# Smaller first transfers and a row read from PSUM: both ends of a two-block decoder kernel

## The chip, the cores and the metric

One core of a Trainium2 chip. The metric is the device time in microseconds (us) of one execution. The engines are TensorE (PE; its weight loads are shown apart as PEld), VectorE (DVE), ScalarE (ACT), GpSimd (POOL) and the sequencer that issues most DMAs (SyncE, SP).

## The reference

Two small language-model blocks, one after the other, on one sequence of 256 tokens with 1024 channels, all in float32. The first block puts 16 meta tokens in front (272 tokens) and has two layers: latent attention (8 heads) and a gated linear recurrence. The second has two layers of attention (differential, then ordinary causal) with a memory attention, and an MLP with a squared relu:

```
h = concatenate([meta, x]);  h = h + mla_mixer(rmsnorm(h, g) @ w_in ...)    # first block
...
u = relu(h @ w_up);  h = h + (u * u) @ w_down                               # end of the last layer
out = rmsnorm(h, final_norm_2) = h * rsqrt(mean(h * h) + 1e-6) * final_norm_2
```

## The kernel before, in words

The residual stream lies in SBUF with channels on partitions: 8 tiles of 128 channels by 272 (later 256) tokens. The weights come from DRAM as 252 units, 512 KB each but for a few, in the order of their use. A weight W is split into a rounded part `weights_hi` (ACT, L1016) and the rest `weights_lo` (DVE, L1449); the input is split likewise (`operand_hi`, `operand_lo`). A product is three matmuls (L666 hi*hi, L667 hi*lo, L668 lo*hi), so a unit of 8 tiles costs TensorE 24 matmuls of 272 or 256 columns. There are 5 buffers for raw units and 6 for split ones; ACT waits before it splits unit v until unit v-6 has been multiplied.

Every engine runs a fixed list of steps. `timetable()` (L240) makes the lists for ACT and DVE by sorting steps by the numbers of the table `TIMES` (L157): a step with the number 8.5 stands between the split of unit 8 and that of unit 9. TensorE's list follows the units, with the statistics and attention steps at fixed places between them. An engine works through its list strictly in order, so a step whose input is late holds all that stand behind it.

Start. SP issues the gains (`vec`), then in turn two input tiles (272 KB) and half a unit (256 KB), four times, then units 2 to 4 and the constants (L2014 to L2023). ACT and DVE split input tiles and weight halves in that order (`input_a`, `split_weights(piece=i)`, L1419 to L1423, L1949 to L1954); then ACT squares the tiles and splits units 2, 3 and 4 in between, while DVE adds the squares up. TensorE multiplies units 0 and 1 (`tile_by_inputs`, L697): for each of two output tiles, over four input tiles. The first norm ("a"): `mean` (L852) on TensorE behind unit 3, `root` (L1048) on ACT, `rstd` on DVE, `spread` (L867) on TensorE behind unit 4, `row` (L1042) on ACT. `row` copies a row of per-token factors from a PSUM bank into SBUF.

End. The last eight units are the `down` projection (L779): output tiles 2j and 2j+1 share a PSUM bank. After each pair DVE adds it to the residual (`residual_pair`), ACT squares it, DVE adds the squares. After the last unit: the same for tiles 6 and 7, `total`, `mean`, `root`, `rstd`, `spread`; ACT multiplies all eight tiles by the gain (L1436 to L1440), copies the row, DVE multiplies three pairs by it, POOL the tiles 6 and 7 one by one, and SP writes five pieces.

## Time and profile before

| | |
|---|---|
| median of 3 runs | 844.8 us (844.73 to 845.4) |
| the profiled execution | 846.0 us, span of its instructions 844.2 us |
| TensorE busy | 818.6 us, 97% of the span, 6612 matmuls |
| DVE / ACT busy | 560.8 us / 532.3 us |
| DMA | 137.39 MB, 163 GB/s over the span |
| first matmul / last residual add | 7.83 us / 832.12 us from the span's start |

Times in the profile count from the span's start. A busy TensorE says only that a matmul was in its pipeline; the pace is the distance between two starts. Idle time of an engine is listed with what ended it.

### The profile page before, as it was taken

The numbers are of one execution on the slowest core, as the hardware profiler recorded it, in microseconds if no ns is written. First come the engines' busy times: TensorE is split into PE (matmuls) and PEld (weight loads), VectorE is DVE, ScalarE is ACT, GpSimd is POOL, SyncE is SP. The second block draws the span as 40 slices with busy tenths as digits, with TensorE's granted clock in tenths as the row PEclk, the third lists the DMA queues.
The fourth block names the chain that finished last, engine by engine and source line by source line (L and its number), as shares of the span: only waits on it lengthen the run. The fifth ranks groups of instructions, "written<-read, shape, count | busy, mean of one in ns | idle before, by whom it ended". The sixth has DMA issues, their size and how long they took to land.

```text
span 844.2 us, 16068 instructions
## 1 busy us (share of the span) xinstructions
PE 818.6 (97%) x6612; PEld 786.2 (93%) x6612; DVE 560.8 (66%) x1004; ACT 532.3 (63%) x962; POOL 2.6 (0%) x6
## 2 busy tenths in 40 slices
PE   6999999999999998899999999999999999999994
PEld 6997769999999898899999999999899999999994
DVE  6685658889988976567536553876758656465353
ACT  6478766589977868763544545668867546444442
POOL 0000000000000000000000000000000000000001
PEclk9999999999999999999999999999999999999998
DMA  8453215555745432445645764444336737374431
GB/s 313 150 188 113 63 51 172 191 162 210 231 170 170 124 124 98 155 171 166 221 163 181 250 193 150 150 151 144 107 108 217 242 119 253 113 258 167 148 101 50
DMA packets 41448, 137.39 MB, mean 163 GB/s; under 512 B 4384, under 2 KB 8736, under 8 KB 41376
## 3 DMA queue, kind: packets, MB, share of 16 engines
q1 hardware_dynamic: 41376, 136.37, 49.0%
q8 instruction: 52, 0.85, 0.4%
q14 instruction: 20, 0.16, 0.1%
HBM read 135.31 MB, written 1.05 MB: 162 GB/s over the span
## 4 chain that ended last, share of the span: by engine, by line
PE 94%; DVE 3%; ACT 1%; DMA 1%; issue 0%; DVEq 0%; ACTq 0%; SPq 0%
PE bank L666 26%; PE bank L668 26%; PE bank L667 25%; PE bank L671 2%; PE bank L939 2%; PE bank L672 2%; PE bank L673 2%; PE bank L891 1%; PE bank L892 1%; DVE temp L1449 1%; PE bank L860 1%; DVE residual L1449 1%; PE bank L919 1%; DMA weights_raw<-stream_dram 1%; PE bank L920 1%; DVE weights_lo L1449 1%
## 5 line engine op out<-in xcount | busy, mean ns | idle before, releaser
L666 PE MATMUL bank<-operand_hi,weights_hi 128*128 128x256 f32 (+1 forms) x1860 | 529.5, 285 | 10.9 <-DVE weights_lo L1449 7.8
L668 PE MATMUL bank<-operand_hi,weights_lo 128*128 128x256 f32 (+1 forms) x1860 | 526.7, 283 | 0.0
L667 PE MATMUL bank<-operand_lo,weights_hi 128*128 128x256 f32 (+1 forms) x1860 | 526.6, 283 | 0.0
L666 PEld LDWEIGHTS bank<-operand_hi,weights_hi 128*128 128x128 f32 x1860 | 352.4, 189 | 16.3 <-DVE weights_lo L1449 8.7
L668 PEld LDWEIGHTS bank<-operand_hi,weights_lo 128*128 128x128 f32 x1860 | 352.8, 190 | 0.0
L667 PEld LDWEIGHTS bank<-operand_lo,weights_hi 128*128 128x128 f32 x1860 | 350.8, 189 | 0.0
L1016 ACT ACTIVATE weights_hi<-weights_raw 128x1024 fp32r<-128x1024 f32 (+2 forms) x254 | 258.3, 1041 | 130.1 <-PE bank L668 92.5
L1449 DVE TENSOR_TENSOR weights_lo<-weights_raw,weights_hi 128x1024 fp32r<-128x1024 f32 (+2 forms) x254 | 298.5, 1205 | 52.5 <-ACT weights_hi L1016 52.4
L1449 DVE TENSOR_TENSOR operand_lo<-temp,operand_hi 128x512 fp32r<-128x512 f32 (+2 forms) x48 | 28.4, 601 | 55.0 <-ACT operand_hi L1016 55.0
L1455 DVE SCALAR_TENSOR_TENSOR temp<-bank,rows 128x512 f32<-128x512 f32 x32 | 21.9, 688 | 40.6 <-PE bank L668 39.7
L671 PE MATMUL bank<-weights_hi,operand_hi 128*128 128x256 f32 (+1 forms) x140 | 41.6, 297 | 0.0
L1028 ACT ACTIVATE temp<-temp 128x512 f32<-128x512 f32 x32 | 19.9, 621 | 33.8 <-DVE temp L1455 33.8
L673 PE MATMUL bank<-weights_hi,operand_lo 128*128 128x256 f32 (+1 forms) x140 | 40.7, 291 | 0.0
L672 PE MATMUL bank<-weights_lo,operand_hi 128*128 128x256 f32 (+1 forms) x140 | 40.6, 290 | 0.0
L1016 ACT ACTIVATE operand_hi<-residual,vectors 128x256 fp32r<-128x256 f32 (+1 forms) x48 | 22.4, 505 | 21.2 <-DVE residual L1449 21.1
L1016 ACT ACTIVATE arena<-bank 128x512 f32<-128x512 f32 (+3 forms) x46 | 22.4, 500 | 19.0 <-PE bank L668 14.1
L1449 DVE TENSOR_TENSOR residual<-residual,bank 128x512 f32<-128x512 f32 (+1 forms) x28 | 17.1, 614 | 25.9 <-PE bank L668 25.6
L1016 ACT ACTIVATE operand_hi<-temp 128x512 fp32r<-128x512 f32 (+2 forms) x48 | 26.7, 560 | 6.2 <-DVE temp L1449 5.1
L1028 ACT ACTIVATE temp<-residual 128x512 f32<-128x512 f32 (+1 forms) x36 | 18.7, 530 | 17.1 <-DVE residual L1449 14.9
L1455 DVE SCALAR_TENSOR_TENSOR operand_lo<-residual,vectors,operand_hi 128x256 fp32r<-128x256 f32 (+1 forms) x48 | 21.5, 486 | 10.8 <-ACT operand_hi L1016 10.7
L1282 ACT ACTIVATE temp<-temp,softmax_stats 128x128 f32<-128x128 f32 (+1 forms) x48 | 21.4, 450 | 11.3 <-DVE softmax_stats L1814 11.3
L671 PEld LDWEIGHTS bank<-weights_hi,operand_hi 128*128 128x128 f32 x140 | 26.4, 188 | 1.5 <-issue 1.0
(177 smaller groups left out, 645.3 us busy)
## 6 DMA issues: line engine op xcount, KB each, us to landing
weights_raw<-stream_dram SPq DMA_DIRECT2D x244, 512.0 KB, 4.4
weights_raw<-stream_dram SPq DMA_DIRECT2D x6, 384.0 KB, 3.5
temp<-memT_dram SPq DMA_DIRECT2D x8, 256.0 KB, 3.4
residual<-xT_dram SPq DMA_DIRECT2D x4, 272.0 KB, 4.9
weights_raw<-stream_dram SPq DMA_DIRECT2D x4, 256.0 KB, 5.1
out_dram<-residual SPq DMA_DIRECT2D x3, 256.0 KB, 2.2
constants<-consts_dram SPq DMA_DIRECT2D x1, 536.0 KB, 7.8
out_dram<-residual SPq DMA_DIRECT2D x2, 128.0 KB, 2.1
```

Source lines behind the costliest of these rows:

```text
L666: e.matmul(to, w_h, x_h, start=start, stop=False, skip_group_check=True)
L667: e.matmul(to, w_h, x_l, start=False, stop=False, skip_group_check=True)
L668: return e.matmul(to, w_l, x_h, start=False, stop=stop, skip_group_check=True)
L671: e.matmul(to, x_h, w_h, start=start, stop=False, skip_group_check=True)
L672: e.matmul(to, x_h, w_l, start=False, stop=False, skip_group_check=True)
L673: return e.matmul(to, x_l, w_h, start=False, stop=stop, skip_group_check=True)
L939: mm = e.matmul(bank[b][:, at:at + nk], qt[p0:p0 + DH, q0:q0 + nq], kt[p0:p0 + DH, 0:nk], start=True, stop=True, skip_group_check=True)
L1016: return e.activation(to, of, ACT.Copy, bias=0.0, **scale)
L1028: return e.activation(to, of, ACT.Square, bias=0.0, scale=scale)
L1282: e.activation(prob[:, at:at + nk], src, ACT.Exp, bias=st[:, 4 * j:4 * j + 1], scale=-1.0, accum_out=st[:, 4 * j + 1:4 * j + 2]).then_inc( ...
L1449: return e.tensor_tensor(to, a, b, op)
L1455: return e.scalar_tensor_tensor(to, a, s, b, op0, op1)
```

## The change

Start: the first input tiles and the first half unit are transferred one by one; the gains and the input tiles 2, 3 and 6, 7 are issued from ACT's own queue, the rest from SP's. A copy of one column on ACT, which needs no input from DRAM, stands ahead of the first input split. TensorE begins with five matmuls of zeros, and in units 0 and 1 the loop over inputs is outside that over the two output tiles. End: tiles 6 and 7 are added and squared one by one (tile 7 in a bank of its own); ACT multiplies by the gain in its list, ahead of and between the last steps; the mean is summed from two parts in PSUM; there is no `row` copy, DVE reads the row from PSUM for four pairs; POOL does nothing; each tile is written on its own, from SP and ACT in turn. Beside that, every number of `TIMES` is new: most steps of ACT and DVE between the splits stand at another place. TensorE's list is the same.

```diff
+WARM = 5
+FIRST_WEIGHTS = [(0, 0, 256), (0, 256, 256), (0, 512, 512), (1, 0, 512), (1, 512, 512)]
+FIRST_TILES = [(0, 1), (1, 1), (2, 2), (4, 2), (6, 2)]
...
+def at_last(w):
+
+    return w.kind == "down" and w.layer == 1 and w.k0 == 24 and w.m0 > 5
...
 TIMES = {
-    ("scalar", "root"): (7.67, 12.29, 12.14, 32.6, 34.67, 74.33, 101.5, 163.67, 194.25),
+    ("scalar", "root"): (8.25, 11.4, 11.8, 33.25, 35.67, 75.33, 99.75, 163.67, 194.33),
...
-    ("vector", "sub_mean"): (87.25, 91.33),
+    ("vector", "sub_mean"): (87.12, 92.25),
...
+    ("scalar", "gained"): (251.23, 251.54, 251.62, 251.46, 251.69, 251.31, 251.77, 251.92),
...
# tile_by_inputs
+                for k in range(4):
+                    pe.wait_ge("weights_piece", first_weights_of(v, k))
+                    wait_input(v, w.k0 + k)
+                    for j, b in enumerate(bank_of(v)):
                         w_h, w_l = weights(v, k, j)
...
+            def mean_out():
+
+                take(6)
+                for k, part in enumerate((temp[0][:, 0:SEQ], temp[2][:, SEQ:512])):
+                    pe.wait_ge(*(("square", "d1", 7) if k else ("total", "out")))
+                    for i in range(2):
+                        mm = e.matmul(bank[6][:, i:i + 1], part[:, i * P:(i + 1) * P], ones[:, 0:1],
+                                      start=k == 0 and i == 0, stop=k == 1, skip_group_check=True)
...
+            pe.wait_ge("zeros")
+            for _ in range(WARM):
+                e.matmul(bank[7][:, 0:SEQ], temp[6][:, 0:P], temp[6][:, P:P + SEQ], start=True, stop=True)
...
# scalar
+            e.dma_start(vec[:], vecs).then_inc(*done("vectors_landed", ("vectors",), by=16))
+            load_tiles(2)
+            act.wait_ge("eps")
+            copy(cols[:, 21:22], EPS_COL, scale=1.0)
+            load_tiles(4)
...
-            for k in range(DT):
-                act.wait_ge("x_added", "d1", k - k % 2)
-                copy(xs[:, k, :], xs[:, k, :], scale=vcol("final_norm_2", k)).then_inc(*done("x_gained", ("x_gained", k)))
-                if k == 1:
-                    root("out")
-            row("out")
+            root("out")
+            for k in range(1, DT, 2):
+                act.wait_ge("out", k - 1)
+                e.dma_start(out[k * P:(k + 1) * P, :], xs[:, k, :]).then_inc(*done("output_written_act", ("written", k), by=16))
...
# vector
+            def residual_last(k):
+                dve.wait_ge("sum", "down", 1, k, 24)
+                tt(xs[:, k, :], xs[:, k, :], bank[3 if k == 6 else 7][:, 0:SEQ], ALU.add).then_inc(
...
-            dve.wait_ge("row", "out")
-            row = RC.unsqueeze(1).to_broadcast([P, 2, SEQ])
-            for k in (0, 2, 4):
-                dve.wait_ge("x_gained", k + 1)
+            dve.wait_ge("spread", "out")
+            row = bank[6][:, P:P + SEQ].unsqueeze(1).to_broadcast([P, 2, SEQ])
+            for k in range(0, DT, 2):
+                for kk in (k, k + 1):
+                    dve.wait_ge("x_gained", kk)
                 tt(xs[:, k:k + 2, :], xs[:, k:k + 2, :], row, ALU.mult).then_inc(*done("outputs", ("out", k)))
```

## Rows read from the trace of the kernel before

**Rows 1.** The page, part 1: engine, busy us, share, instructions.

```profile
PE 818.6 (97%) x6612; PEld 786.2 (93%) x6612; DVE 560.8 (66%) x1004; ACT 532.3 (63%) x962; POOL 2.6 (0%) x6
```

**Rows 2.** The page, part 4: shares of the chain that ended last, by engine.

```profile
PE 94%; DVE 3%; ACT 1%; DMA 1%; issue 0%; DVEq 0%; ACTq 0%; SPq 0%
```

**Rows 3.** Waits of TensorE, 60 to 832 us, first and last of six: total us, times, longest.

```profile
PE bank L666 <- DVE operand_lo L1455: 3.1, 3, 1.7
...
PE bank L891 <- ACT arena L1016: 0.5, 1, 0.5
```

**Rows 4.** Timeline of the start: start us, duration, engine, line, what [idle before].

```profile
4.30 1.28 ACT L1016 ACT_TABLE_LOAD   x1 [4.30 <-DMA residual<-xT_dram]
5.18 0.67 SPq L1994 DMA_DIRECT2D weights_raw<-stream_dram  x1
7.83 0.59 PE L666 MATMUL bank<-operand_hi,weights_hi 128*128 128x272 f32 x1 [7.83 <-DVE weights_lo L1449]
```

**Rows 5.** DMA issued at 5.18 us (unit 2): KB, us to landing.

```profile
weights_raw<-stream_dram SPq DMA_DIRECT2D x1, 512.0 KB, 6.4
```

**Rows 6.** Chain of waits, start of the kernel: start us, us, what.

```profile
8.42 0.23 PE bank L667
13.83 0.13 PE bank L667
```

**Rows 7.** Timeline of ACT and DVE, 11 to 26 us.

```profile
11.69 1.04 ACT L1016 ACTIVATE weights_hi<-weights_raw 128x1024 fp32r<-128x1024 f32 x1
17.55 0.43 ACT L1028 ACTIVATE temp<-residual 128x272 f32<-128x272 f32 x1 [1.07 <-DVE temp L1449]
17.89 3.89 ACT L1016 ACTIVATE weights_hi<-weights_raw 128x1024 fp32r<-128x1024 f32 x4
...
11.37 0.68 DVE L1449 TENSOR_TENSOR weights_lo<-weights_raw,weights_hi 128x512 fp32r<-128x512 f32 x1
12.84 1.23 DVE L1449 TENSOR_TENSOR weights_lo<-weights_raw,weights_hi 128x1024 fp32r<-128x1024 f32 x1 [0.43 <-ACT weights_hi L1016]
15.94 1.23 DVE L1449 TENSOR_TENSOR weights_lo<-weights_raw,weights_hi 128x1024 fp32r<-128x1024 f32 x1 [0.51 <-ACT weights_hi L1016]
```

**Rows 8.** Timeline of TensorE: start of unit 2, mean and spread of norm "a".

```profile
16.57 0.29 PE L666 MATMUL bank<-operand_hi,weights_hi 128*128 128x272 f32 x1
...
22.62 0.72 PE L860 MATMUL bank<-constants,temp 128*128 128x1 f32 x6
23.20 0.37 PE L666 MATMUL bank<-operand_hi,weights_hi 128*128 128x272 f32 x1
...
26.41 0.59 PE L876 MATMUL bank<-constants,cols 16*128 16x16 f32 x3
```

**Rows 9.** Chain of waits: a float32 matmul of 272 columns, two instructions.

```profile
69.50 0.65 PE bank L892 x2
```

**Rows 10.** Groups of DVE, 0 to 832 us: busy us, mean ns of one | idle.

```profile
L1449 DVE TENSOR_TENSOR residual<-residual,bank 128x272 f32<-128x272 f32 x8 | 3.5, 435 | 2.1 <-PE bank L668 2.0
```

**Rows 11.** Timeline of the end, all engines.

```profile
832.12 0.69 DVE L1449 TENSOR_TENSOR residual<-residual,bank 128x512 f32<-128x512 f32 x1 [3.60 <-PE bank L668]
834.71 0.61 PE L860 MATMUL bank<-constants,temp 128*128 128x1 f32 x4 [2.70 <-DVE temp L1449]
835.36 0.26 ACT L1059 ACTIVATE cols<-bank,cols 128x2 f32<-128x2 f32 x1 [1.08 <-PE bank L860]
835.96 0.44 PE L876 MATMUL bank<-constants,cols 128*128 128x128 f32 x2 [0.64 <-DVE cols L1513]
838.30 0.69 DVE L1449 TENSOR_TENSOR residual<-residual,rows 128x512 f32<-128x512 f32 x1 [2.49 <-ACT rows L1016]
838.35 1.23 POOL L1986 TENSOR_TENSOR residual<-residual,rows 128x256 f32<-128x256 f32 x1 [837.91 <-ACTq L472]
838.91 1.21 DVE L1449 TENSOR_TENSOR residual<-residual,rows 128x512 f32<-128x512 f32 x1
```

**Rows 12.** Page, part 6: output DMAs, KB each, us to landing.

```profile
out_dram<-residual SPq DMA_DIRECT2D x2, 128.0 KB, 2.1
```

More of the change, by code:

```diff
@@ L403, in timetable @@
             vector("finish", v)
+    end = AT["down", 1, 24, 0]
+    for m in range(8):
+        scalar("gained", m)
+    vector("total_out")
     return {engine: [step for _, _, step in sorted(rows)] for engine, rows in table.items()}
@@ L593, in bank_of @@
             if w.kind == "down":
-                return [w.m0 // 2]
+                return [7 if w.layer == 1 and w.m0 == 7 else w.m0 // 2]
             if w.kind == "up":
@@ L709, in tile_by_inputs @@
                                   w.k0 + k == 0, w.k0 + k == 7)
-                    i.then_inc(*done("sums", ("sum", w.kind, w.layer, j), ("unit", v)))
-                    held_by[b] = [("evacuated", w.kind, w.layer, j)]
+                        if k == 3:
+                            i.then_inc(*done("sums", ("sum", w.kind, w.layer, j), ("unit", v)))
+                            held_by[b] = [("evacuated", w.kind, w.layer, j)]
             def tiles(v, T, t0=0, base=0):
@@ L782, in down @@
                 pe.wait_ge("weights_lo", v)
-                (b,), j = bank_of(v), w.m0 % 2
+                (b,), j = bank_of(v), 0 if w.layer == 1 and w.m0 == 7 else w.m0 % 2
                 if w.k0 == 0 and j == 0:
@@ L865, in mean @@
                     mean("in2_0g")
+            def mean_out():
[5 more added lines that the diff above has]
+                                      start=k == 0 and i == 0, stop=k == 1, skip_group_check=True)
+                mm.then_inc(*done("statistics_sums", ("mean", "out")))
+                held_by[6] = [("mean_read", "out")]
             def spread(name):
@@ L1239, in squares_pair, with d1_squares, last_squares, gained @@
                 square(pair(to), xs[:, m:m + 2, :]).then_inc(*done("squares", ("square", name, m)))
+            def d1_squares(m):
+                act.wait_ge("x_added", "d1", m)
+                squares_pair("d1", m)
+            def last_squares(k):
+                act.wait_ge("x_added", "d1", k)
+                act.wait_ge("square_read", "d1", 4)
+                square(temp[2][:, (k - 6) * SEQ:(k - 5) * SEQ], xs[:, k, :]).then_inc(
+                    *done("squares", ("square", "d1", k)))
+            def gained(k):
+                act.wait_ge("square", "d1", k if k > 5 else k - k % 2)
+                copy(xs[:, k, :], xs[:, k, :], scale=vcol("final_norm_2", k)).then_inc(*done("x_gained", ("x_gained", k)))
             def squares_gained(m):
@@ L1757, in residual_pair, with total_out @@
                     *done("residual", ("x_added", name, m), ("evacuated", step[0], step[1], m + 1)))
+            def residual_last(k):
+                dve.wait_ge("sum", "down", 1, k, 24)
+                tt(xs[:, k, :], xs[:, k, :], bank[3 if k == 6 else 7][:, 0:SEQ], ALU.add).then_inc(
+                    *done("residual", ("x_added", "d1", k), ("evacuated", "down", 1, k)))
+            def total_out():
+                dve.wait_ge("square_read", "d1", 4)
+                linked(tt(temp[0][:, 0:SEQ], temp[0][:, 0:SEQ], temp[0][:, SEQ:512], ALU.add))
+                dve.wait_ge("square", "d1", 6)
+                tt(temp[0][:, 0:SEQ], temp[0][:, 0:SEQ], temp[2][:, 0:SEQ], ALU.add).then_inc(
+                    *done("square_sums", ("total", "out")))
             def residual_pair_rest(name, m, o, gain, *ready):
@@ L1946, in bank_of_tile @@
                 return m if m < 2 else bank_of(AT["a_in", 0, 0, m])[0]
+            e.memset(temp[6][:, 0:P + SEQ], 0.0).then_inc(*done("statistics", ("zeros",)))
             e.memset(EPS_COL, EPS).then_inc(*done("statistics", ("eps",)))
@@ L2029, in sync @@
                 load_weights(v)
[L2030 to L2031 removed]
+            for k in range(0, DT, 2):
                 sp.wait_ge("out", k)
[L2033 removed]
+                load(out[k * P:(k + 1) * P, :], xs[:, k, :], "output_written",
                      "written", k)
[L2035 removed]
+            sp.wait_ge("written", 6)
         tally.begin(known=False)
[L2039 removed]
+        for body in (sync, scalar, vector, tensor):
             body(Rehearsal())
```

200 lines of the change are left out of this document (103 added, 97 removed), and 36 rows, old and new, of the table TIMES.

## The prediction

> **What bounds the kernel now.** I read the page first. TensorE is busy 97% of the span [rows 1] and makes up 94% of the chain that ended last [rows 2], so between the ends time is the pace of its matmuls, which the change leaves alone. The waits of TensorE come next: between 60 and 832 us there are eight, in six rows of which the first and the last stand in [rows 3]; with 0.8, 0.8, 0.7 and 0.5 us of the four between they come to 6.4 us, the longest 1.7. That is all that a new order of ACT's and DVE's steps could win back there. Then the two ends. At the start TensorE stands still for 7.83 us; ACT waits until 4.30 us for the first input tiles and only then loads its function table, 1.28 us [rows 4]. After the start the pace is 0.23 us a matmul, later 0.13 us [rows 6]: 272 columns in 0.227 us are 1.2 GHz, in 0.125 us nearly 2.4 GHz; it changes near 13.5 us, 5.7 us after the first matmul. At the end, 12.1 us of the span (844.2 - 832.12) lie behind the last residual add [rows 11].
>
> **The start, until unit 2.** The first input tile is now 136 KB at the head of its queue, and the table load lies beside its transfer, so ACT can begin near 3.5 us instead of 5.60. The table load (1.28 us) and most of a us of landing go. But TensorE has to be followed to where it next runs without waiting. Unit 2 is issued at 5.18 us and lands 6.4 us later, at 11.6 [rows 4, 5]; ACT splits it at 11.69, 1.04 us, DVE from 12.84 to 14.07 [rows 7]. Nothing of the bytes ahead of it has changed (gains, eight tiles, units 0 and 1 come to 2.2 MB either way), so I leave 14.07 as it is. TensorE began unit 2 at 16.57 [rows 8]. It can now begin at 14.1, if units 0 and 1 are through: 2.5 us gained, no more.
>
> Are they through? Their last piece was split by 12.05 (11.37 + 0.68) [rows 7]; with ACT's earlier start I take 11.6. It feeds 12 matmuls, 1.5 us at 0.125: done at 13.1. That needs the fast pace. The five matmuls of zeros start near 1.1 us. A float32 matmul of 272 columns took 0.65 us at the fast pace [rows 9], so one of 256 takes 0.61, and up to 1.22 at the slow one: together 3.1 to 6.1 us. The trace shows none at the slow pace; the ordinary matmul grew 1.8 times, which gives 5.5 us, until 6.6. If the clock rises again 5.7 us after the first activity, it does so near 6.9 and nothing of units 0 and 1 is late. If the zeros do not count, real matmuls start at 6.6, 31 of the 48 run at 0.227 until 13.6, the other 17 end at 15.7: 0.9 us gained. The loop turned round costs nothing by itself (same 48 matmuls) and lets TensorE use a piece as it comes.
>
> The Trainium skill, "DMA: Bandwidth & Descriptors", section "Issuing engines are not separate DMA queues", says that DMAs of several issuers interleave on the same 16 engines, and that a second issuer saves only issue time. It speaks against a gain from the second queue; since the sum above takes none for unit 2, it is the same by that rule. The section "Bandwidth" adds that small transfers move fewer bytes a second; no row here compares 136 with 272 KB. If it cost unit 2's landing half a us, the start would win that much less.
>
> **The start, after unit 2.** Unit 3 is ready at 17.17 (15.94 + 1.23) [rows 7]; TensorE wants it at 14.07 + 3.02 = 17.09: 0.1 us lost. It ends at 20.2, `mean` takes 0.58 (22.62 to 23.20), unit 4 takes 3.21 (23.20 to 26.41) [rows 8]: TensorE wants `spread` at 24.0. Here the new list bites. `root` of norm "a" stood ahead of the split of unit 8 (7.67), now behind it (8.25). ACT splits units 4 to 7 from 17.89 to 21.78 without a pause [rows 7]; unit 8 at that rate (0.95 each) ends at 22.7. Table load 1.28 [rows 4], root 0.26 and 0.34 from its end to the start of the spread, as at the end of the kernel (835.62 to 835.96) [rows 11]: `spread` at 24.6 against 26.41, a gain of 1.8 us. DVE's split of unit 7 waits behind `rstd`, but is wanted only at 31. ACT's copy of the row follows at once, so the banks of units 0 and 1 are free before unit 6 wants one. Behind that everything is relative to TensorE. **Start: 1.8 us**; bounds 0.9 - 0.6 = 0.3 (clock low and ACT late) and 2.9 (unit 2 lands 0.4 earlier, root in time).
>
> **The middle.** Nothing is added for TensorE. A step of ACT or DVE moved by one split comes about 1.0 us (ACT) or 1.2 us (DVE) earlier or later [rows 7]. The lists move both ways: `sub_mean` of the second group from 91.33 to 92.25, behind unit 92's split; `root` of norm "in2_0" from 74.33 to 75.33; but the first memory softmax on DVE from 74.67 to 73.5. TensorE waits only where a chain is short of time, and the eight waits follow directly on work that TensorE itself had just finished, so much of each is plain latency that no order removes. I take zero; bounds: half of the waits gone (-3.2), three more splits in front of a wait (+3.2).
>
> **The end.** From 832.12, in the new order: add of one tile 0.44 [rows 10]; square of one tile on ACT 0.43, as at 17.55 [rows 7]; two matmuls of the mean 0.61, the first part having been summed under the last unit's wake; root 0.26; 0.34 to the spread, 0.44 for it [rows 11]. With five handovers of 0.03 that is 834.8, against 838.30 for DVE's first product before. What goes: half an add, half a square, the two sums of squares (833.5 to 834.7) and, the largest, the wait for ACT's six gain copies and the row copy: the spread was there at 836.4, DVE began at 838.30. These copies now lie under the last unit: five of them 2.1 us between unit 250's square and the end, the eighth behind the last square and beside the mean, so `root` is not held. Then four products instead of three with two on POOL. DVE's product took 0.69 alone and 1.21 beside POOL's [rows 11]; one that reads PSUM took 0.69 too (the add at 832.12), so four take 2.5 us at a pitch of 0.60 (838.30 to 838.91): 837.3. The last two tiles go out on two queues, landing 2.1 us after the issue [rows 12], 839.4; the span ended 0.4 us behind the last landing: 839.8 against 844.2. **End: 4.4 us.** Bounds: 3.4 (an ACT-issued write lands half a us later and the tiny matmuls run at the low clock, as they did when the row shows 0.44 at 835.96) and 4.9 (smaller pieces land sooner).
>
> **Sum.** 1.8 + 0 + 4.4 = 6.2 us. The profiled execution took 846.0 us, span 844.2; the same 6.2 off the median of the runs, 844.8, gives 838.6.
>
> **Rivals.**
> 1. *The new lists also shorten TensorE's waits.* For: 6.4 us are there [rows 3], and steps such as the first softmax stand earlier. Against: each wait follows a handover chain of its own. Half of them: 838.6 - 3.2 = 835.4.
> 2. *The start gives nearly nothing*: clock low through units 0 and 1, as computed 0.9 instead of 2.5 us, and ACT late for `root`: 844.8 - 4.4 - 0.3 = 840.1. The Trainium skill, "TensorE: Matmul & The Clock Gate", section "The HAM clock gate", says that activity releases the throttle; by that rule the zeros count and this rival falls; the rows show only a rise 5.7 us behind the first matmul.
> 3. *The lists cost a part of the gain*, one to four splits in front of waiting steps (1 to 5 us): about 841.6.
> 4. *Slower.* One split more in front of the step that TensorE waits for, at each of the eight places of rows 3 (units 18 to 97, the attention of the layers): 8 x 1.05 = 8.4 us against 6.2, 847.0. It decides from six places on. For: `sub_mean` 91.33 to 92.25 and `root` 74.33 to 75.33 are such moves. Against: others go the other way.
> 5. *The smaller first transfers do not land sooner*: ACT then starts at 4.3, and unit 2 still sets the pace; the time stays within 0.3 us of the forecast, so it has no case of its own.
>
> **How the numbers follow.** Forecast 0.52, rival 1 0.18, rival 2 0.12, rival 3 0.12, rival 4 0.06. The forecast alone would lie in 837.3 to 839.9. The range reaches to rival 1 and rival 3: 835.0 to 841.8. About 0.2% (1.7 us) can be told from no change. Faster needs more than 1.7 of 6.2 us to stay: all cases but rival 4 and the worst of rival 3. Faster 0.92, same 0.03, slower 0.05.
>
> **What would show it.** Unit 2 begins near 14.1 us and `spread` of norm "a" near 24.6; the pace at the first real matmul 0.125 us (else rival 2). Between unit 5 and the last, the same distance as before, with eight waits of about 6 us. From the last add to the end 7.7 us, DVE's first product 2.6 us behind the add and no product above 0.7 us. I am wrong if the waits of TensorE in the middle differ from 6.4 us by more than 1, or if unit 2 lands well ahead of 11.6.

## The result and the profile after

| | before | after |
|---|---|---|
| median of the runs | 845.3 us (6 runs, 844.73 to 845.76) | 840.2 us (6 runs, 838.93 to 841.47) |
| profiled execution, its span | 846.0, 844.2 us | 838.93, 837.1 us |
| mean granted clock of the span | .995 | .997 |
| TensorE waits between unit 5 and the last | 6.4 us, eight | 6.0 us, nine |
| last residual add to the span's end | 12.1 us | 8.1 us |

The ratio is 0.9941, interval [0.9926, 0.9955]: 0.6% faster, clear of the interval, and inside the forecast's range; the forecast was 838.6. The six runs of the changed kernel do not lie around their median. Three have spans of 837.0 to 837.4 us, three of 839.4 to 839.5, with nothing between. The profile is one of the short ones, so it shows 7.1 us less span where the medians differ by 5.1. Both numbers need an explanation.

First the start: ACT's part of the timeline. Columns: start, duration, engine and line, operation, what it waited for.

```profile
0.73 0.41 ACTq L1482 DMA_DIRECT2D vectors<-vecs_dram  x1
...
1.65 1.28 ACT L1061 ACT_TABLE_LOAD   x1 [1.65 <-PEq L2207]
...
3.98 0.52 ACT L1061 ACTIVATE operand_hi<-residual,vectors 128x272 fp32r<-128x272 f32 x1 [0.83 <-DMA vectors<-vecs_dram]
4.41 0.40 ACT L1061 ACTIVATE weights_hi<-weights_raw 128x256 fp32r<-128x256 f32 x1
6.11 0.52 ACT L1061 ACTIVATE operand_hi<-residual,vectors 128x272 fp32r<-128x272 f32 x1 [1.30 <-DMA residual<-xT_dram]
6.87 0.42 ACT L1061 ACTIVATE weights_hi<-weights_raw 128x256 fp32r<-128x256 f32 x1 [0.23 <-DMA weights_raw<-stream_dram]
...
11.23 0.74 ACT L1073 ACTIVATE temp<-residual 128x272 f32<-128x272 f32 x2
11.87 1.04 ACT L1061 ACTIVATE weights_hi<-weights_raw 128x1024 fp32r<-128x1024 f32 x1
```

The table load has left the path [rows 4]. The first split waits for the gains, not for the input tile: issued at 0.73 us from ACT's queue, beside the tile on SP's, they land 3.2 us later, where the same 79 KB took 1.9 us before, first on SP's queue. That costs little: ACT then waits 1.30 us more for the second tile and 0.23 us for the second piece of weights, issued at 2.10 and landed at 6.84. From 6.87 on ACT works without a pause. It comes to unit 2 at 11.87 because its own list ends there; the unit had landed near 11.0. TensorE and the two views of the first norm:

```profile
5.52 0.39 PE L694 MATMUL bank<-operand_hi,weights_hi 128*128 128x272 f32 x1
...
7.79 0.40 PE L694 MATMUL bank<-operand_hi,weights_hi 128*128 128x272 f32 x1 [1.26 <-DVE weights_lo L1516]
...
9.41 0.39 PE L694 MATMUL bank<-operand_hi,weights_hi 128*128 128x272 f32 x1 [0.59 <-DVE weights_lo L1516]
...
20.52 0.72 PE L890 MATMUL bank<-constants,temp 128*128 128x1 f32 x6
24.82 0.56 PE L917 MATMUL bank<-constants,cols 16*128 16x16 f32 x3 [0.45 <-DVE cols L1580]
```

```profile
18.06 4.83 ACT L1061 ACTIVATE weights_hi<-weights_raw 128x1024 fp32r<-128x1024 f32 x5
22.91 1.28 ACT L1104 ACT_TABLE_LOAD   x1
24.20 0.26 ACT L1104 ACTIVATE cols<-bank,cols 128x3 f32<-128x3 f32 x1
```

Unit 2 began at 14.29 (16.57 before), `mean` at 20.52 (22.62), `spread` at 24.82 (26.41) [rows 8]. In the second fence ACT splits five units on end, unit 8 as the last, before it loads the table for `root`; TensorE waits for that at 24.82.

The middle, the list of TensorE's waits (total, times, longest), the two top rows:

```profile
PE bank L694 <- DVE operand_lo L1522: 2.3, 2, 1.7
PE bank L980 <- DVE softmax_stats L1894: 0.8, 1, 0.8
```

In [rows 3] the first was 3.1 us in three waits. The wait that is gone stood in front of the first `up` units; in the kernel before:

```profile
366.84 0.39 PE L666 MATMUL bank<-operand_hi,weights_hi 128*128 128x256 f32 x1 [0.79 <-DVE operand_lo L1455]
```

Two waits of 0.2 us are new. The end:

```profile
828.96 0.42 DVE L1516 TENSOR_TENSOR residual<-residual,bank 128x256 f32<-128x256 f32 x1 [1.37 <-PE bank L696]
829.41 0.42 ACT L1073 ACTIVATE temp<-residual 128x256 f32<-128x256 f32 x1 [0.35 <-DVE residual L1516]
...
829.88 0.61 PE L903 MATMUL bank<-constants,temp 128*128 128x1 f32 x4 [0.62 <-ACT temp L1073]
830.52 0.26 ACT L1104 ACTIVATE cols<-bank,cols 128x2 f32<-128x2 f32 x1 [0.16 <-PE bank L903]
830.82 0.17 DVE L1580 RECIPROCAL cols<-cols 128x2 f32<-128x2 f32 x1 [1.44 <-ACT cols L1104]
...
831.13 0.49 PE L917 MATMUL bank<-constants,cols 128*128 128x128 f32 x2 [0.64 <-DVE cols L1580]
831.66 2.48 DVE L1516 TENSOR_TENSOR residual<-residual,bank 128x512 f32<-128x512 f32 x4 [0.68 <-PE bank L917]
832.37 2.12 SPq L2068 DMA_DIRECT2D out_dram<-residual  x4
832.38 2.16 ACTq L1507 DMA_DIRECT2D out_dram<-residual  x4
```

It answers to [rows 11]: from the add to DVE's first product 2.7 us (6.2 before), and no product waits for a row copy.

To see where the time comes from, both traces are cut at points that both kernels have: `mean` of a norm, which follows the same unit in both (the last cut is the last residual add).

| stretch | before | after | gained |
|---|---|---|---|
| span's start to `mean` of norm a | 22.62 | 20.52 | 2.10 |
| to `mean` of norm q | 13.30 | 13.78 | -0.48 |
| to `mean` of norm mlp_0 | 333.18 | 332.04 | 1.14 |
| to `mean` of norm mlp_1 | 286.06 | 285.72 | 0.34 |
| to the last add | 176.96 | 176.90 | 0.06 |
| to the span's end | 12.08 | 8.14 | 3.94 |

So start 1.6, middle 1.5, end 3.9: 7.1 us.

### The profile page after: what moved, and what is told of

Its sections match the earlier page's. It is cut to its first block, busy times and chain, and to the rows that moved or that the text cites. A ratio compares the mean times of both kernels' runs of the same rounds, so it can differ in the third digit from the quotient of the medians.

```text
span 837.1 us, 16103 instructions
## 1 busy us (share of the span) xinstructions
PE 820.2 (98%) x6626; PEld 786.6 (94%) x6626; DVE 561.4 (67%) x1008; ACT 531.9 (64%) x964; POOL 0.2 (0%) x4
## 4 chain that ended last, share of the span: by engine, by line
PE 82%; ACT 8%; DVE 6%; issue 2%; DMA 1%; DVEq 0%; SPq 0%; ACTq 0%
PE bank L694 23%; PE bank L696 23%; PE bank L695 23%; ACT weights_hi L1061 2%; PE bank L980 2%; DVE weights_lo L1516 1%; PE bank L699 1%; PE bank L700 1%; PE bank L701 1%; ACT operand_hi L1061 1%; DMA weights_raw<-stream_dram 1%; PE bank L932 1%; PE bank L933 1%; DVE arena L1516 1%; DVE temp L1516 1%
## 5 line engine op out<-in xcount | busy, mean ns | idle before, releaser
L1061 ACT ACTIVATE weights_hi<-weights_raw 128x1024 fp32r<-128x1024 f32 (+3 forms) x255 | 258.5, 1039 | 148.5 <-PE bank L696 107.4
L1516 DVE TENSOR_TENSOR weights_lo<-weights_raw,weights_hi 128x1024 fp32r<-128x1024 f32 (+3 forms) x255 | 298.7, 1199 | 42.9 <-ACT weights_hi L1061 42.4
L1516 DVE TENSOR_TENSOR residual<-residual,bank 128x512 f32<-128x512 f32 (+2 forms) x33 | 19.8, 609 | 23.6 <-PE bank L696 22.7
L1073 ACT ACTIVATE temp<-residual 128x512 f32<-128x512 f32 (+2 forms) x37 | 19.0, 521 | 17.2 <-DVE residual L1516 15.0
L1522 DVE SCALAR_TENSOR_TENSOR operand_lo<-residual,vectors,operand_hi 128x256 fp32r<-128x256 f32 (+1 forms) x48 | 21.7, 486 | 10.3 <-ACT operand_hi L1061 10.1
```

What stands on the lines that cost most here:

```text
L1061: return e.activation(to, of, ACT.Copy, bias=0.0, **scale)
L1073: return e.activation(to, of, ACT.Square, bias=0.0, scale=scale)
L1516: return e.tensor_tensor(to, a, b, op)
L1522: return e.scalar_tensor_tensor(to, a, s, b, op0, op1)
```

## The experiments

Ratios are to the kernel before on the same chip. Since spans scatter by 2 to 3 us while most of the questions are about less, the cuts above, read in each profiled execution, carry most verdicts.

**1. The kernel again.** No edit.

> The changed kernel once more, nothing altered. Its six runs fell in two groups: three with a span of 837.0 to 837.4 us and a granted clock of .996 to .997, three with 839.4 to 839.5 us and .994. Theory A (clock at the start): in the longer runs TensorE is held at the low level for some 4 us more of the first 10 us, perhaps in the gaps of 1.4 and 0.75 us in which it waits for inputs after the matmuls of zeros; .997 less .994 of 837 us at half clock is 5 us of low time, which costs 2 to 2.5 us. Then the groups return, 837 and 839.4, nothing in between, and no version with more zeros or without gaps has both. Theory B (other place, for instance one eviction or wait in the middle): the groups return as well, but a profile of a longer run shows the full clock from 5.3 us on and the loss elsewhere.

Median 839.65 us, ratio 0.9923 [0.9906, 0.9941]; spans 837.0, 837.1, 837.1, 838.2, 838.7, 839.1: the short ones return, the gap behind them doesn't. The profile fell on the 838.7. Below are stretches of that execution (from:to, length, TensorE busy and matmuls in it, granted clock, DMA share, GB/s), and the same of the first profile of this kernel:

```profile
core 0 of [0], span 838.7 us
...
5.00:9.40 4.40, 3.08 (x15) 1.00 1.05 374
...
324.00:327.60 3.60, 2.16 (x16) 0.99 0.00 0
327.60:331.00 3.40, 3.40 (x17) 0.51 0.03 11
```

```profile
core 0 of [0], span 837.1 us
...
324.00:327.60 3.60, 2.15 (x16) 1.00 0.00 0
327.60:331.00 3.40, 3.40 (x30) 1.00 0.14 14
```

17 matmuls instead of 30 in the same 3.4 us: TensorE was held at 1.2 GHz there, not at 2.4. What it did before: in the 3.6 us ahead it was busy for 2.16, with the two waits of 0.8 us for the scores of the differential heads. The cut around it, from `mean` of norm in2_0 to that of mlp_0, is 109.31 us against 107.86: 1.45 us longer. Theory A had the place wrong (the start held here), and B was right for this execution. But A's place comes in the next ones.

**2. The old lists in the middle.** The tables of ACT and DVE as before, save the steps of the last eight units.

```diff
-    ("scalar", "root"): (8.25, 11.4, 11.8, 33.25, 35.67, 75.33, 99.75, 163.67, 194.33),
+    ("scalar", "root"): (7.67, 12.29, 12.14, 32.6, 34.67, 74.33, 101.5, 163.67, 194.25),
...
```

> Both ends as changed, but ACT's and DVE's lists between them are those of the kernel before (only the steps of the last eight units keep their new places). The trace of the changed kernel gives 1.55 us of its gain to the middle (end of start gain 1.6 at the first spread, last add 3.16 us earlier). Theory L (the lists are worth it): the first spread comes at 24.3 to 24.4, since root of norm a stands ahead of unit 8's split again (0.5 us gained), and the middle loses 1.5 us, the waits of TensorE back at 6.4 us: 1.0 us longer than the changed kernel. Theory M (the middle's 1.5 us are not the lists but the earlier start or chance): 0.5 us shorter than the changed kernel. Forecast: L, ratio to the kernel before .995 to .996 against .994 for the changed kernel.

Median 841.19, ratio 0.9936 [0.9915, 0.9957], profile 838.5 us. From `mean` of norm a to q 13.30 us, as theory L said. From there to mlp_1 618.42 us against 617.76 (617.4 to 617.8 in the eight other executions with the new lists and no low stretch there), 619.24 before. The wait in front of the first `up` unit is back:

```profile
365.53 0.39 PE L668 MATMUL bank<-operand_hi,weights_hi 128*128 128x256 f32 x1 [0.30 <-DVE operand_lo L1496]
```

So the lists give at least 0.7 us of the middle's 1.5, half of what theory L said; the other 0.8 lies between two executions with the same old lists. More than half of that can be placed. From the last matmul ahead of the first `up` unit to its first one it is 1.07 us in the kernel before, 0.58 here, and 0.12 in all twelve executions with the new lists: the old lists leave a wait there whose length varies, and the new ones end it. For the remaining 0.3 us no cause is shown. Theory L had the waits back at 6.4 us; they were 5.9. And the clock fell at the start: up at 5.7 us, down again from 9.07 to 12.49; `mean` of norm a came at 21.85 instead of 20.52. (The second piece of weights was 0.7 us later too; see the table behind experiment 12.)

**3. The old start** on the new lists and the new end.

```diff
-FIRST_WEIGHTS = [(0, 0, 256), (0, 256, 256), (0, 512, 512), (1, 0, 512), (1, 512, 512)]
-FIRST_TILES = [(0, 1), (1, 1), (2, 2), (4, 2), (6, 2)]
+FIRST_WEIGHTS = [(0, 0, 512), (0, 512, 512), (1, 0, 512), (1, 512, 512)]
+FIRST_TILES = [(0, 2), (2, 2), (4, 2), (6, 2)]
...
-            e.dma_start(vec[:], vecs).then_inc(*done("vectors_landed", ("vectors",), by=16))
-            load_tiles(2)
-            copy(cols[:, 21:22], EPS_COL, scale=1.0)
-            load_tiles(4)
...
-            for _ in range(WARM):
-                e.matmul(bank[7][:, 0:SEQ], temp[6][:, 0:P], temp[6][:, P:P + SEQ], start=True, stop=True)
```

> The changed kernel with the start of the kernel before: gains, tile pairs and half units from one queue, no early copy for the function table, no zeros, units 0 and 1 looped by outputs. The lists and the end stay. Theory S (the start is worth the 1.6 us that the first spread moved): the time is 1.6 us above the changed kernel's quick group, 840.6 us of execution, spread at 26.4 to 27 (root now stands behind unit 8's split, which cost nothing here if unit 8 is split by 24), and there is one group only, since the clock then rises where it did before. If the two groups of the changed kernel come from somewhere other than the start, they stay, 2.3 us apart. Rival (the start is worth little, since a later wait would have caught it): within 0.5 us.

Median 839.98, ratio 0.9928 [0.9907, 0.9948], spans 836.9, 837.9, 837.9, 838.2, 838.3, 840.5: no difference from the changed kernel that can be told, the shortest span included (837.0 there). Theory S asked for 1.6 us. `spread` at 26.34, as before, so in this execution the old start did cost 1.5 us against the first profile; the clock rose once, at 13.4 us. The whole new start shows neither in the median nor in the shortest span.

**4. The old end** on the new start and lists.

```diff
-            root("out")
...
+            for k in range(DT):
+                act.wait_ge("x_added", "d1", k - k % 2)
+                copy(xs[:, k, :], xs[:, k, :], scale=vcol("final_norm_2", k)).then_inc(*done("x_gained", ("x_gained", k)))
+                if k == 1:
+                    root("out")
+            row("out")
```

> The changed kernel's start and lists with the end of the kernel before: tiles 6 and 7 as a pair, gain copies and row copy behind the last add, POOL for two products, five writes from one queue. Theory E: the end costs the 3.9 to 4.0 us that last add to span end shrank by (12.08 to 8.1): 841.0 us in the quick group, and the two groups stay (the start is the new one), 841.0 and 843.3. Rival: less than 3.4 us, if the last unit's own list (gain copies under unit 251) had slowed the splits there.

Median 844.22 of 12 runs, ratio 0.9978 [0.9965, 0.999]. Shortest spans 841.1 against 837.0; last add to the end 12.0 us (829.69 to 841.7) against 8.1. Theory E stands: 3.9 to 4.1 us, and it is the one part whose undoing is clear of the intervals.

**5. `root` in front of unit 8's split.**

```diff
-    ("scalar", "root"): (8.25, 11.4, ...
+    ("scalar", "root"): (7.9, 11.4, ...
```

> The changed kernel with one number of the list altered: root of norm a at 7.9 instead of 8.25, so it stands ahead of ACT's split of unit 8 again. The prediction's step: root waited for nothing but that split. In the changed kernel mean starts at 20.5 us and spread at 24.82; the traces with root ahead of the split take 13.30 us from mean of norm a to mean of norm q, the changed kernel 13.78. Theory R: spread comes 0.48 us earlier relative to mean, at 24.35, the split of unit 8 about 1.6 us later without a wait for it, and the whole kernel is 0.5 us shorter (quick runs: span 836.5 to 836.9). Rival: TensorE waits for unit 8's weights or for the bank instead, and the 0.5 us is given back before unit 13.

Median 839.69, ratio 0.9916 [0.9892, 0.9941]; shortest spans 836.4 and 836.6. From `mean` of a to `mean` of q 13.30 us, as said, but see below. The timeline of ACT there shows the order that this buys:

```profile
22.46 1.28 ACT L1078 ACT_TABLE_LOAD   x1
23.76 0.26 ACT L1078 ACTIVATE cols<-bank,cols 128x3 f32<-128x3 f32 x1
23.92 1.05 ACT L1035 ACTIVATE weights_hi<-weights_raw 128x1024 fp32r<-128x1024 f32 x1
```

Unit 8 is split behind `root`, TensorE runs into `spread` without a wait, and nothing later waits for unit 8, as theory R has it. But in this execution the clock had fallen from 9.42 to 12.83, and TensorE came late by itself (`spread` at 25.68): 11, with a like fall and `root` still behind the split, took 13.30 us too. So the 0.5 us is not shown by this stretch. What speaks for it: the wait of 0.45 us ahead of `spread` in the first profile, shortest spans 0.4 to 0.6 us below 837.0, and 10 against 7, both without a fall, 34.63 against 34.91 us at `mean` of q: 0.3 us.

**6. Zeros in the gaps too.**

```diff
                             held_by[b] = [("evacuated", w.kind, w.layer, j)]
+                    if v == 0:
+                        zeros((2, 1, 0, 0)[k])
```

> The changed kernel with three more matmuls of zeros, which nothing reads: two behind the first six real ones of unit 0 and one behind the next six, each 0.6 us, to fill the gaps of 1.4 and 0.75 us in which the clock may fall. Theory G (the gaps make the clock fall): after the rise at 5 to 7 us no run falls back before 20 us; unit 2 starts at 14.2 to 14.5 in the profile, and the slower runs that come from the start (low from 8.4 or 9.1 to 11.8 or 12.5 us, 1.3 us lost) are gone, while low stretches in the middle, as at 327 us, remain (span 837 or 838.7). Rival H (the fall depends on something else): the same spread of spans, 837 to 839.5, in about the same shares. If the fillers come too late they hold the real matmuls by up to 0.3 us.

Median 840.59, ratio 0.9931 [0.9908, 0.9954], spans 837.1 to 839.9. The profile shows no fall at the start, `mean` at 20.91 (0.4 us later than in the first profile, and so was the second piece of weights, at 7.26 against 6.87, so the fillers are not shown to cost anything), and one in the middle, at the same place as in 1 (327.8 to 331.2). One profile can't tell whether the start now always holds; the scatter is as wide as ever. Inconclusive, and of no use for the time. What the fillers do is shorten TensorE's first wait behind the zeros to 0.15 us.

**7. No zeros.** `WARM = 0`.

> The changed kernel without the five matmuls of zeros. By the prediction's working TensorE then runs units 0 and 1 largely at the low clock: first real matmul at 5.5 us at 0.227 us, rise between 11 and 13 us, unit 2 at 15.2 to 15.6 instead of 14.29, spread about 1.1 us later, quick runs 838.2 instead of 837.1. Theory Z: so it is. Rival: unit 2 and spread are bound by ACT anyway (root behind unit 8's split, itself behind the split of unit 2 and the squares): then spread loses nothing or less than 0.5 us, and the zeros bought little; the old start, whose clock rose only at 13.4, lost 1.3 to 1.5 us against the new one.

Median 839.28, ratio 0.992 [0.9897, 0.9943]; spans 836.7 to 837.5 and one of 839.8. The first matmul ran at 5.40 us at the slow pace, the clock rose at 11.5, `mean` came at 20.98, `spread` at 25.44: 0.46 and 0.6 us later than in the first profile, where the expectation had 1.1. The rival is nearer. What TensorE loses at the slow pace in units 0 and 1 it partly makes good in the waits of 1.3 and 0.6 us that it otherwise has there.

**8. The gain copies behind `root` again,** all else of the new end kept.

```diff
+            for k in range(DT):
+                gained(k)
+                if k == 1:
+                    root("out")
-            root("out")
```

> The changed kernel with ACT's eight gain copies where they stood before: none under the last unit, two ahead of root and six behind it; all else of the end as changed (row read from PSUM, single tiles, two queues). The prediction called these copies together with the row copy the largest part of the end's gain, 1.9 us. Copies take 0.39 to 0.43 us. Theory P: root waits for the first two (0.4 to 0.8 us), the last copy ends 6 x 0.42 = 2.5 us behind root, near 834.0, so the last product ends near 835.0 instead of 834.14: the end is 0.9 to 1.3 us longer, spans 838.1 to 838.4 in quick runs. Rival (the copies were the wait, nearly 2 us): 839.0.

Median 839.16, ratio 0.9917 [0.9895, 0.9939]; last add to the end 8.0 us (828.99 to 837.0), against 8.1 with the copies under the last unit. Both theories fell:

```profile
830.56 0.26 ACT L1075 ACTIVATE cols<-bank,cols 128x2 f32<-128x2 f32 x1
830.71 2.09 ACT L1032 ACTIVATE residual<-residual,vectors 128x256 f32<-128x256 f32 x5
...
831.60 2.48 DVE L1490 TENSOR_TENSOR residual<-residual,bank 128x512 f32<-128x512 f32 x4 [0.59 <-ACT residual L1032]
```

The copies start 0.9 us before DVE's products and stay ahead of them to the end; `root` isn't held by the first two either, since they lie beside the `mean`.

**9. `root` first, and zero-value work in the middle.** Fillers in front of the two waits at 324 and 326 us.

```diff
             def scores(layer, kind, h):
                 b = 3 + h % 2
+                if layer == 0 and kind == "diff" and h in (8, 10):
+                    for step in held_by.get(7, ()):
+                        pe.wait_ge(*step)
+                    e.matmul(bank[7][:, 0:SEQ], const[:, 0:P], const[:, 0:SEQ], start=True, stop=True)
```

> root of norm a at 7.9, as in root_first, and two float32 matmuls of 256 columns over constants, whose result nothing reads, ahead of the scores of differential heads 8 and 10: there TensorE waits 0.93 and 1.0 us on DVE, and two of the profiled runs had their clock fall just behind (low from 327.5 to 330.9 us and from 327.8 to 331.2 us, 1.5 us lost). Theory G (waits of TensorE that stand close together make the clock fall): the middle low stretch is gone in all runs; those at the start (8 to 12.8 us) stay. Spans 836.4 to 838.1, none above 838.5; median 838.9 of execution. Rival H (chance, or heat): runs with a span of 838.5 to 839.5 are still there, a low stretch somewhere in the middle. Each filler may cost 0 to 0.2 us if it overlaps the released matmuls.

Median 840.94, ratio 0.9933 [0.9917, 0.995]; spans 836.3, 836.8, then 838.5 to 839.8. The profile is one of the long ones (839.4), and its loss is at the start:

```profile
5.00:9.40 4.40, 2.67 (x15) 0.99 1.03 354
9.40:12.80 3.40, 2.84 (x13) 0.50 1.03 423
12.80:16.20 3.40, 3.40 (x17) 0.51 1.03 414
16.20:20.00 3.80, 3.80 (x32) 1.00 0.77 275
```

In the first profile of the changed kernel the middle two stretches held 27 matmuls each. `mean` of norm a came at 23.46 us, later than in the kernel before. The stretch from in2_0 to mlp_0 took 107.81 us, without a fall, and the fillers cost it nothing; but it had none in eight of ten profiled executions with the new lists and no fillers either, so they are not shown to help. The expectation had no span above 838.5; three were.

**10. The same without the zeros at the start.**

> The same without the five matmuls of zeros at the start. no_zeros started spread at 25.44 against 24.82, with the clock rising once at 11.51 us and never back; the zeros let it rise at 5 to 6.6 us, but three of seven profiled executions with zeros and the new start saw it fall again for 3.4 us. Theory Z2 (zeros win 0.5 us when the clock holds and lose as much or more when it falls): the fast end of the spans is 836.7 to 836.9 (0.3 to 0.5 above root_and_fill's 836.4), the median equal within 0.3 us, the scatter smaller. Rival: with root in front, spread no longer waits for ACT, so the whole later start of units 0 and 1 shows: 0.9 us longer in every quick run.

Median 839.59, ratio 0.9925 [0.9913, 0.9938]; five spans of 837.5 to 838.2, the narrowest of all, shortest 1.2 us above those of 9. The clock rose once, at 12.05 us; `mean` at 21.34, `spread` at 25.12. With `root` in front, more of TensorE's own start shows, as the rival had it; against 9, the median is 1.4 us better, inside the intervals. Here the zeros give a better best case with a wider scatter; but with `root` behind the split the shortest span was 836.7 without zeros (7) and 837.0 with them, so a better best case is not shown for them in general.

**11. Only the row from PSUM,** on 4's old end: no row copy, DVE does all four products.

```diff
-            dve.wait_ge("row", "out")
-            row = RC.unsqueeze(1).to_broadcast([P, 2, SEQ])
-            for k in (0, 2, 4):
+            dve.wait_ge("spread", "out")
+            row = bank[7][:, P:P + SEQ].unsqueeze(1).to_broadcast([P, 2, SEQ])
+            for k in (0, 2, 4, 6):
```

> end_undone with one thing of the new end: DVE reads the row of factors from PSUM and does all four pairs; no row copy on ACT, nothing on POOL, four writes of pairs. The six gain copies stay between root and the end. gains_late showed that their place costs nothing; so of the end's 4.0 us the part that the prediction put down to gain copies and row copy together (1.8 us: spread's matmul at 836.4, first product 838.30 before) should all be the row copy, which stood behind six gain copies in ACT's list. Theory C: first product 0.1 us behind the spread, last product ends 2.2 us earlier relative to the last add, the time from mean of the last norm to the end 2.2 us shorter than in end_undone: span 839.0 to 839.3 in quick runs against 841.1 to 841.4. Rival (DVE needs POOL's help, or PSUM reads cost more): 1.2 us or less.

Ratio 0.9953 [0.9939, 0.9967] against 0.9978 for 4. Last add to the end 9.7 us (831.46 to 841.2) against 12.0: 2.3 us, theory C's 2.2. The two ends, first with the row copy, then without:

```profile
833.09 2.49 ACT L1012 ACTIVATE residual<-residual,vectors 128x256 f32<-128x256 f32 x6
...
833.53 0.40 PE L868 MATMUL bank<-constants,cols 128*128 128x128 f32 x2 [0.64 <-DVE cols L1519]
835.48 0.36 ACT L1012 ACTIVATE rows<-bank 128x256 f32<-128x256 f32 x1
835.87 2.95 DVE L1455 TENSOR_TENSOR residual<-residual,rows 128x512 f32<-128x512 f32 x3 [2.49 <-ACT rows L1012]
```

```profile
834.86 2.49 ACT L1012 ACTIVATE residual<-residual,vectors 128x256 f32<-128x256 f32 x6
...
835.30 0.40 PE L868 MATMUL bank<-constants,cols 128*128 128x128 f32 x2 [0.64 <-DVE cols L1518]
835.74 2.48 DVE L1454 TENSOR_TENSOR residual<-residual,bank 128x512 f32<-128x512 f32 x4 [0.59 <-ACT residual L1012]
```

The gain copies stand at the same place in both. The row copy of 0.36 us waited behind six of them in ACT's list, and all products waited behind it. The start of the spread to the first product is 2.34 us with the copy and 0.44 without: 1.9 us of the 2.3. The other 0.4 to 0.5 us is the products themselves, four on DVE alone in 2.48 us against three in 2.95 beside POOL's two. Whether a row copy put ahead of the gain copies would have done as well was not tried. This execution had two low stretches, 10.1 to 13.5 us and 122.8 to 126.2; the second is 1.57 us in the cut around it (107.54 against 105.97).

**12. All output tiles from SP's queue.**

```diff
-            for k in range(1, DT, 2):
-                act.wait_ge("out", k - 1)
-                e.dma_start(out[k * P:(k + 1) * P, :], xs[:, k, :]).then_inc(*done("output_written_act", ("written", k), by=16))
```

> The changed kernel with all eight output tiles written from SP's queue, none from ACT's. In the changed kernel the issues take 0.53 us each (SP 832.37, four in 2.12 us), and the last product ends at 834.14. Theory Q (two queues save issue time): eight issues on one engine from 832.37 take 4.2 us, the last at 836.1 instead of 834.1, so the end is 1.7 to 2.0 us later: span 838.8 to 839.1 in quick runs. Rival (the writes are bound by the DMA engines or by the products): within 0.4 us of the changed kernel's 837.0.

Median 840.14, ratio 0.994 [0.9922, 0.9958], shortest span 837.5. Last add to the end 8.9 us (829.02 to 837.9):

```profile
832.35 3.78 SPq L2064 DMA_DIRECT2D out_dram<-residual  x8
```

The last issue ends at 836.13, 1.6 us later than with two queues, yet the end moves by 0.74 only: between Q and its rival. Eight issues on end took 0.47 us each; the 0.53 of the expectation was a stretch of four issues with the waits for products in it.

**The start over all profiled executions** (us from the span's start; "low again" is the clock's fall after its first rise, "second piece" the start of ACT's split of the second piece of weights, "first wait" TensorE's first wait behind the zeros, in us):

| execution | zeros | first rise | low again | second piece | first wait | `mean` a | `mean` q |
|---|---|---|---|---|---|---|---|
| before | no | 13.6 | no | - | - | 22.62 | 35.92 |
| 3, old start | no | 13.4 | no | - | - | 22.55 | 35.85 |
| 7 | no | 11.5 | no | 6.80 | - | 20.98 | 34.91 |
| 10, root first | no | 12.1 | no | 7.01 | - | 21.34 | 34.63 |
| after | yes | 5.3 | no | 6.87 | 1.26 | 20.52 | 34.30 |
| 1 | yes | 6.6 | no | 6.95 | 0.81 | 20.60 | 34.39 |
| 12 | yes | 4.2 | no | 6.60 | 1.23 | 20.25 | 34.41 |
| 6, gaps filled | yes | 6.9 | no | 7.26 | 0.15 | 20.91 | 34.70 |
| 8 | yes | 4.7 | 8.1-11.5 | 7.01 | 1.80 | 21.11 | 34.44 |
| 4 | yes | 5.0 | 8.4-11.8 | 7.74 | 2.37 | 21.63 | 35.17 |
| 2, old lists | yes | 5.7 | 9.1-12.5 | 7.58 | 1.89 | 21.85 | 35.15 |
| 5, root first | yes | 6.0 | 9.4-12.8 | 7.36 | 1.50 | 21.89 | 35.19 |
| 11 | yes | 6.7 | 10.1-13.5 | 7.25 | 1.09 | 21.98 | 35.28 |
| 9, root first | yes | 5.9 | 9.3-16.2 | 7.55 | 1.73 | 23.46 | 36.75 |

"First rise" is where the matmuls come to the fast pace; the listed clock stands at 1.00 before it too (in the kernel before from 7.83 to 13.50 us, at the pace of 0.227), so a mean clock doesn't count the slow start. With zeros, and without the fillers of 6, the clock fell again in six of nine executions; without zeros, in none of four. These are few: if the zeros had no part in it, such a split would still come up about once in 20. The earliest fall cost least (execution 8), the longest most (9).

The columns on the second piece and the first wait say more. The second piece of weights, issued at 2.1 us, lands at another time in each execution, 1.1 us apart at most. ACT waits for it, and comes to unit 2 5.0 us after it began that piece, in all ten executions with zeros and in 7 and 10. Where the clock held, TensorE began unit 2 within 0.06 us of the end of its split (14.03 to 14.69 us): there this landing, through ACT's list, sets the start. Where it fell, TensorE was 0.5 to 1.3 us behind that end, once 2.5 us, and without zeros 0.7 to 0.9 us: this is what the clock costs there. A late landing also lengthens the first wait. That was 0.15 to 1.26 us where the clock held and 1.50 to 2.37 us in five of the six where it fell; execution 11, with 1.09 us, is the exception. So the falls go with longer waits behind the zeros, but one execution shows that the length of this wait alone doesn't decide.

By `mean` of q the new start is worth 1.5 to 1.6 us when the clock holds (35.92 - 34.30; 1.2 in 6), 0.6 to 1.5 us when it falls for the shorter time, and cost 0.8 us once. It is worth 1.0 us without zeros, 1.3 with `root` in front as well. Which part of it gives this isn't shown: the zeros and the place of `root` were varied alone, but the smaller transfers, the early table load, ACT's queue and the turned loop only together (3).

## Why the prediction came out right, step by step

**Start, 1.8 us forecast.** 1.6 us in the first profile; `spread` at 24.82 for 24.6, unit 2 at 14.29 for 14.1. The number for unit 2 is right for a wrong reason: the step "unit 2 is issued at 5.18 us and lands 6.4 us later" held it to the landing. The unit was issued at 4.86 and landed near 11.0, 0.6 us ahead of what the prediction held fixed (a mild case of its own sign of being wrong), since ACT had taken two tile pairs and the gains off SP's list; what set 14.29 was ACT's own list, which can't go on before the second piece of weights (6.84 us here, 6.6 to 7.7 in the others) and then has no slack until 11.87. The prediction has no such term. The step on `root` behind unit 8's split was right: TensorE waited 0.45 us for it ahead of `spread`; from the runs, moving it is worth 0.3 to 0.6 us at best. All this is one execution against one. In the medians the start gives nothing that can be told (experiment 3), so the 1.8 us is not confirmed as a gain in time.

**The clock.** The forecast took the rise for settled once it had come. This step failed: six of nine starts with zeros had the clock fall again. The prediction weighed rival 2 (clock low through units 0 and 1) as one case with 0.12; a low clock came in more than half of the executions with zeros, at 0.5 to 1.3 us each and 2.5 once (read at the start of unit 2). The rule that I took from the Trainium skill ("TensorE: Matmul & The Clock Gate", "The HAM clock gate"), activity releases the throttle, agrees with every first rise in the table; that it would stay released through the waits behind the zeros (1.1 to 2.4 us for the first one, where it fell) was my addition. The delay wasn't constant either: 2.9 to 5.6 us from the first matmul of zeros (1.31 us) to the rise, 5.6 to 6.4 from the first real one without zeros, where one value, 5.7, was taken. And the zeros took 4.4 us, not 5.5. No run here shows what exactly decides rise or fall.

**Middle, 0 forecast.** 1.5 us gained in the traces, within the bounds of 3.2, but the zero was a term mis-sized. Experiment 2 gives 0.7 us of it to the lists, and up to 1.2 with the varying wait at the `up` units: a part of rival 1. The two added waits are of 0.2 us, so rivals 3 and 4 fell. The waits went from 6.4 to 6.0 us, and only the one before the `up` units vanished, as the argument of plain latency has it for the others.

**End, 4.4 us forecast.** 3.9 us. First product 2.7 us behind the add (forecast 2.7 from the terms, said as 2.6), last product's end 5.2 behind it (834.14 - 828.96; forecast 5.2). The missing 0.45 us lies behind the last product: 3.0 us to the span's end, where 2.5 had been taken; writes from ACT took 2.3 us to land and those from SP 2.1, and the rest is in the span's last instructions. The bound of 3.4 covers it. In the working, "the largest, the wait for ACT's six gain copies and the row copy" named two things as one. Experiments 8 and 11 part them: the gain copies' place is worth nothing once no row copy stands behind them; the row copy is worth 1.9 us, and another 0.4 comes with POOL's products gone. The second queue is worth 0.7 us; if these add up, that leaves 0.9 us for single tiles and the mean in two parts together, which I did not part further.

**Sum.** 6.2 forecast, 7.1 between the profiles, 5.1 and 6.3 between medians (first comparison, experiment 1), 0.6% to 0.8% of the time. Low stretches can account for the difference: where they were profiled they take 1.5 us each in the middle and 0.5 to 2.5 us at the start. For the long executions of the first comparison, and for the kernel before (spans from 842.4 to 848.2 us, mean clocks of .996 to .989), only the mean clock speaks for them. The changed kernel's spans of 837.0 to 837.4 us have .996 to .998, those of 838.7 to 839.5 have .994. The mean is a rough sign: one of 838.2 has .998, and it also counts the low clock behind the last units, 5.8 us in the first profile but 2.9 in experiment 8's, which had a fall at the start and still shows .996.

Undone one at a time on one chip, the start, the lists and the end put the median 0.3, 1.5 and 4.6 us above the changed kernel's, together 6.4 of its gain of 6.3 there; the first two are inside the intervals. The forecast had 1.8, 0 and 4.4. By these numbers the end was forecast well, and the total came near because the start gave less than forecast and the lists more. That the two misses cancel is luck.

None of the variants is faster than the changed kernel beyond its interval. The best candidate is `root` first, with the shortest spans (836.3 and 836.4); its 0.3 to 0.6 us are not clear of the scatter.

## What to carry to other kernels

A small copy that stands behind a batch in an in-order list costs the batch, not itself: look at what is queued ahead of it before you credit the batch. Here a row needed only for the last products was cheaper to read in PSUM than to copy. And when runs of one kernel lie in groups, compare the granted clock of both executions stretch by stretch before you explain the difference by an edit: a profile of the short group overstates the gain (7.1 against 5.1 us here).

## What the runs showed of the hardware

- After TensorE's clock had risen, it fell to half again, ahead of the end, in 8 of 14 profiled executions: six times at the start behind the zeros, three times in the middle (twice near 327 us, behind two waits of 0.8 us, once at 122.8, 1.0 us behind the end of a wait of 0.5 us), at 1.45 to 1.57 us each there. At the start the first wait behind the zeros had been 1.1 to 2.4 us where the clock fell, 0.15 to 1.26 where it held. The same waits in the middle passed without a fall in most executions.
- The 79 KB of gains landed 1.9 us after the issue when they went first from the one queue (2.0 in 3), 2.6 to 3.3 us when an input tile was issued at the same time from another. The Trainium skill, "DMA: Bandwidth & Descriptors", section "Issuing engines are not separate DMA queues", says that DMAs of several issuers interleave on the same engines; the trace agrees.
- A weight piece of 128 KB issued at 2.1 us, among the other first transfers, landed 4.5 to 5.6 us later, differently in each execution.
- DVE's product of two tiles by a row in PSUM took a pitch of 0.60 us, four in 2.48 us; with the row in SBUF the first step was 0.61 us as well (838.30 to 838.91), the later products 1.21 us each beside POOL's.
